# Attention heads scheduled by half after each value chunk, two start-up tables loaded from another queue, one row turn a unit earlier

## The reference, cut to what matters

```python
qkv = (h @ w_qkv).reshape(b, rows, GRID_W, 3, N_HEADS, HEAD_DIM)
q = qkv[0] * (1.0 / math.sqrt(HEAD_DIM));  k = qkv[1];  v = qkv[2]
scores = einsum(q_r, k_band) + relative bias, masked to a window
p = softmax(scores);  out = einsum(p, v_band)
x = x + out @ w_o
```

## Time and profile before

| what | value |
|---|---|
| median of 3 runs | 2391.72 us |
| the profiled execution | 2390.82 us |
| its span, first to last instruction | 2389.0 us |
| PE busy | 2336.6 us (98% of the span) |
| DVE busy | 1747.0 us (73%) |
| ACT busy | 1358.9 us (57%) |
| DMA | 397.43 MB, mean 166 GB/s |
| mean granted TensorE clock | 0.996 |
| PE's share of the chain that ended last | 72% (DVE 22%, issue 3%, ACT 3%) |

### The profile page before, as it was taken

How to read it: one execution, slowest core, us unless ns; L and a number is a source line. 1 busy time by engine, 2 the same in 40 slices (tenths; PEclk the granted TensorE clock), 3 DMA queues, 4 the chain that set the end, 5 groups by cost and what they waited for, 6 DMA issues and landing times.

```text
span 2389.0 us, 45199 instructions
## 1 busy us (share of the span) xinstructions
PE 2336.6 (98%) x15648; PEld 2092.1 (88%) x15648; DVE 1747.0 (73%) x3166; ACT 1358.9 (57%) x2527; POOL 42.8 (2%) x86
## 2 busy tenths in 40 slices
PE   8999999999999999999999999999999999899998
PEld 8899999999888888899999999988888887688776
DVE  5667999899755555775999899965556577667565
ACT  5655555877555555445445677755555455665554
POOL 1000000000000000000000000000000000000000
PEclk9999999999999999999999999999999999999999
DMA  7355555444566666555555544566665653246454
GB/s 242 126 175 159 169 167 167 149 141 139 178 192 192 194 193 192 168 178 175 177 173 169 154 141 141 155 199 193 201 198 176 185 171 105 71 124 196 130 158 142
DMA packets 137336, 397.43 MB, mean 166 GB/s; under 512 B 12464, under 2 KB 13808, under 8 KB 136432
## 3 DMA queue, kind: packets, MB, share of 16 engines
q1 hardware_dynamic: 134432, 384.97, 52.3%
q0 software_dynamic: 2480, 10.57, 1.3%
q10 hardware_dynamic: 288, 0.10, 0.0%
HBM read 394.54 MB, written 1.05 MB: 166 GB/s over the span
## 4 chain that ended last, share of the span: by engine, by line
PE 72%; DVE 22%; issue 3%; ACT 3%; DMA 0%; DVEq 0%; ACTq 0%; POOLq 0%; POOL 0%; SPq 0%
PE bank L1015 28%; PE bank L999 14%; PE bank L897 12%; DVE wl L1720 8%; PE bank L903 7%; PE bank L1028 4%; DVE arena L1931 1%; DVE arena L1932 1%; DVE arena L1934 1%; PE bank L956 1%; DVE arena L1933 1%; ACT wh L1335 1%; PE bank L944 1%; DVE arena L1930 1%; DVE arena L2003 1%
## 5 line engine op out<-in xcount | busy, mean ns | idle before, releaser
L1720 DVE TENSOR_TENSOR wl<-raw,wh 128x1024 fp32r<-128x1024 f32 (+1 forms) x732 | 893.6, 1222 | 492.0 <-ACT wh L1335 477.4
L1335 ACT ACTIVATE wh<-raw 128x1024 fp32r<-128x1024 f32 (+1 forms) x732 | 771.8, 1055 | 626.5 <-PE bank L1015 337.4
L999 PE MATMUL bank<-xh,wh 128*128 128x256 f32 x2048 | 512.6, 288 | 0.0
L999 PE MATMUL bank<-xl,wh 128*128 128x256 f32 x2048 | 501.5, 283 | 0.0
L999 PEld LDWEIGHTS bank<-xh,wh 128*128 128x128 f32 x2048 | 391.8, 191 | 1.4
L999 PEld LDWEIGHTS bank<-xl,wh 128*128 128x128 f32 x2048 | 392.6, 192 | 0.0
L999 PE MATMUL bank<-xh,wl 128*128 128x256 f32 x2048 | 292.6, 285 | 13.2 <-DVE wl L1720 13.2
L999 PEld LDWEIGHTS bank<-xh,wl 128*128 128x128 f32 x2048 | 262.7, 191 | 20.2 <-DVE wl L1720 18.9
L1015 PE MATMUL bank<-wh,gl 128*128 128x512 f32 x1008 | 270.1, 390 | 1.7 <-DVE gl L2058 1.7
L1015 PE MATMUL bank<-wh,gh 128*128 128x512 f32 x1008 | 269.8, 389 | 0.5 <-ACT gh L1501 0.5
L1015 PE MATMUL bank<-wl,gh 128*128 128x512 f32 x1008 | 269.5, 389 | 0.0
(11 more groups left out here) (296 smaller groups left out, 2739.2 us busy)
## 6 DMA issues: line engine op xcount, KB each, us to landing
raw<-in_w_upT SPq DMA_DIRECT2D x256, 512.0 KB, 3.5
raw<-in_w_down SPq DMA_DIRECT2D x256, 512.0 KB, 3.5
raw<-in_l_w_in SPq DMA_DIRECT2D x84, 512.0 KB, 3.6
raw<-in_peer_w_query SPq DMA_DIRECT2D x32, 512.0 KB, 4.2
raw<-in_l_w_out SPq DMA_DIRECT2D x28, 512.0 KB, 3.8
raw<-in_attn_w_qkv SPq DMA_DIRECT2D x24, 512.0 KB, 4.3
raw<-in_conv_w_in SPq DMA_DIRECT2D x24, 512.0 KB, 3.8
arena<-in_na_bias POOLq DMA_DIRECT2D x4, 1024.0 KB, 5.6
```

The costliest lines, as they stand in the source:

```text
L999: last = pe.matmul(banks[b][:, 0:SEQ], lhsT=w[part][:, k, :], rhs=x_in[xp][:, k, :], start=(k == 0 and part == 0 and xp == 0), stop=(k == ...
L1335: act.activation(wh[:, n % SPLIT, 0:kts * cols], raw[:, n % RAW, 0:kts * cols], ACT.Copy)\
L1720: tt(wl[:, n % SPLIT, 0:kts * cols], raw[:, n % RAW, 0:kts * cols], wh[:, n % SPLIT, 0:kts * cols].bitcast(F32), ALU.subtract).then_inc(lo ...
```

## The change

**Order of chunks.** `QKV_CHUNKS` becomes q0, k0, v0, q1, k1, v1. Chunks 2 and 5 are now the value chunks (copied by ACT), 0, 1, 3, 4 are q and k (copied by DVE).

**Steps of heads.** Heads 0 to 7 have one S per unit in units 9 to 16, T two units later, O one unit after that (12 to 19). Heads 8 to 15 have two S per unit in units 21 to 24, T one unit later (22 to 25), and O in units 24 (four heads), 25 and 26. The turns for `wo` stand at 17, 20, 25 and 27.

**Buffers.** The turned weights go to 6 buffers in `aux`, and the sums to `small`.

**The two start-up tables** are issued by POOL ahead of everything else that POOL does, and share one semaphore. PE's first transpose and DVE's first operation wait for both.

**The convolution's row turn** stands after unit 2 (`ROWS_EARLY`), and DVE's copy with it.

```diff
@@ -63,11 +63,11 @@
 SPLITS = ("attn", "peer0", "rescaled0", "conv", "peer1", "rescaled1", "mem", "even", "odd")
 SCALES = ("mem",)
 ROW_SCALES = ("attn", "peer0", "conv", "peer1", "mem", "between", "even", "odd", "final")
-WO_TURN, OUT_TURN, EVEN_TURN, ROWS_AFTER, ROWS_EARLY, ROWS_CONV = 30, 1, 2, 7, 2, 3
+WO_TURN, OUT_TURN, EVEN_TURN, ROWS_AFTER, ROWS_EARLY = 30, 1, 2, 7, 2
 
 
 ARENA = 32768
-L_QT, L_KT, L_V, L_BIAS, L_O, L_OT, L_PT = 0, 2048, 4096, 6144, 14336, 16384, 20480
+L_QT, L_KT, L_V, L_BIAS, L_O, L_OT = 0, 2048, 4096, 6144, 14336, 16384
 P_LOW = 16384
 P_QT, P_SC, P_KEYS, P_TOP = P_LOW, P_LOW + 4096, P_LOW + 8192, P_LOW + 10240
 C_C, C_U, C_Y, C_YT = 2048, 4096, 8192, 10240
@@ -221,13 +221,13 @@
 ODD_YT = (8, 0, 1, 2, 3, 4, 5, 6, 7)
 ODD_LATE = {2: (7, 8)}
 CONV_CHUNKS = (2, 4, 0, 3, 5, 1)
-QKV_CHUNKS = (0, 2, 1, 3, 4, 5)
+QKV_CHUNKS = (0, 2, 4, 1, 3, 5)
 WO_ORDER = ((0, 0), (1, 0), (0, 1), (1, 1), (0, 2), (0, 3), (1, 2), (1, 3))
 QKV_UNITS = 24
-NA_S = tuple(9 + a // 2 * 2 for a in range(NA_HEADS))
-NA_T = tuple(NA_S[a] + 1 + a % 2 for a in range(NA_HEADS))
-NA_O = tuple(20 + a // 2 if a < 8 else (24, 25, 26)[max(0, a // 2 - 5)] for a in range(NA_HEADS))
-NA_JOINED = (22, 24, 26, 27)
+NA_S = tuple(9 + a if a < 8 else 21 + (a - 8) // 2 for a in range(NA_HEADS))
+NA_T = tuple(NA_S[a] + (2 if a < 8 else 1) for a in range(NA_HEADS))
+NA_O = tuple(NA_T[a] + 1 if a < 8 else max(NA_T[a] + 1, 24) for a in range(NA_HEADS))
+NA_JOINED = (17, 20, 25, 27)
 NA = [(kind, a) for n in range(QKV_UNITS + 8) for kind, at in (("S", NA_S), ("T", NA_T), ("O", NA_O))
       for a in range(NA_HEADS) if at[a] == n]
 
@@ -482,7 +482,7 @@
 
         const_loaded = sem("const_loaded")
         N_CONST = 12
-        ident_loaded, gains_loaded = sem("identity_loaded"), sem("gains_loaded")
+        norm_loaded = sem("identity_and_gains_loaded")
         x_loaded = [sem(f"x{t}_loaded") for t in range(TT)]
         half_done = sem("down_first_half_done")
         landed = [sem(f"raw{s}_landed") for s in range(RAW)]
@@ -538,8 +538,7 @@
         XG = split_groups()
         s_buf = aux_view(0, 3, TT, SEQ)
         pT_buf = aux_view(1536, 2, 2 * TT, P)
-        na_s, na_pT = aux_view(0, 6, TT, SEQ), view(L_PT, NA_HEADS, 2 * TT, P)
-        na_sums = aux_view(3072, NA_HEADS, TT)
+        na_s, na_pT = aux_view(0, 6, TT, SEQ), aux_view(3072, 6, 2 * TT, P)
         ev_s, ev_pT = aux_view(0, 4, TT, SEQ), aux_view(5408, 4, 2 * TT, P)
 
         def scores_of(name, n):
@@ -548,12 +547,12 @@
 
         def turned_of(name, n):
 
-            return {"na": na_pT[:, n % NA_HEADS], "ev": ev_pT[:, n % 4], "om": pT_buf[:, n % 2]}[name]
+            return {"na": na_pT[:, n % 6], "ev": ev_pT[:, n % 4], "om": pT_buf[:, n % 2]}[name]
 
         def sums_of(name, n):
 
             at = 16 + n % 4 * 2 if name == "om" else 38 + n % 8 * 2
-            return na_sums[:, n] if name == "na" else small[:, at:at + 2]
+            return small[:, at:at + 2]
 
         gain_bc = aux_view(2560, D)
         causal = aux_view(3584, TT, SEQ)
@@ -706,6 +705,9 @@
             def const(dst, src):
                 pool.dma_start(dst, src).then_inc(const_loaded, 16)
 
+            pool.dma_start(ident[:], d["c_ident"]).then_inc(norm_loaded, 16)
+            pool.dma_start(gains[:], d["gains"]).then_inc(norm_loaded, 16)
+
             def summed_up(ins):
                 ins.then_inc(summed, 1)
                 pool.wait_ge(summed, count("summed"))
@@ -834,7 +836,7 @@
                     if after:
                         pe.wait_ge(residual_ready, 4 * (RES[after] - 1) + g + 1)
                     elif g == 0:
-                        pe.wait_ge(ident_loaded, 16)
+                        pe.wait_ge(norm_loaded, 16 * 2)
                     if not after:
                         pe.wait_ge(x_loaded[t], 16)
                     for k in range(4):
@@ -1240,11 +1242,11 @@
                     kind, a = NA[k]
                     if (kind, a) == ("S", 0):
                         pe.wait_ge(const_loaded, 16 * N_CONST)
-                        pe.wait_ge(gains_loaded, 16)
+                        pe.wait_ge(norm_loaded, 16 * 2)
                     if a % 8 == 0 and kind in "SO":
-                        for c in (2 * (a // 8), 2 * (a // 8) + 1) if kind == "S" else (4 + a // 8,):
+                        for c in (0, 1) if kind == "S" else (2,):
                             for i in range(2):
-                                wait_read(pe, J.of("qkv", 2 * c + i))
+                                wait_read(pe, J.of("qkv", 2 * (3 * (a // 8) + c) + i))
                     attention("na", NA, na_heads, head_base["na"], [k])
                 for g in range(4):
                     if NA_JOINED[g] == n:
@@ -1256,7 +1258,7 @@
                         done(last, j)
 
             for c in range(6):
-                project("qkv", "TTTTNN"[c], x_in, k=2 * c, ready=norm_parts("attn"), after=lambda u: na_unit(4 * c + u))
+                project("qkv", "TTNTTN"[c], x_in, k=2 * c, ready=norm_parts("attn"), after=lambda u: na_unit(4 * c + u))
             def wo_unit(i):
                 na_unit(QKV_UNITS + i)
                 if QKV_UNITS + i == WO_TURN:
@@ -1270,7 +1272,7 @@
                 def conv_unit(u):
                     if 4 * c + u == 0:
                         turn("conv", "peer0", (2, 3))
-                    elif 4 * c + u == ROWS_CONV:
+                    elif 4 * c + u == ROWS_EARLY:
                         turn_rows("rows_conv", "conv")
 
                 project("conv_in", "T", x_in, k=2 * c, ready=norm_parts("conv"), after=conv_unit)
@@ -1590,8 +1592,6 @@
 
                 return lambda p: act.wait_ge(residual_ready, 4 * (RES[name] - 1) + p)
 
-            act.dma_start(ident[:], d["c_ident"]).then_inc(ident_loaded, 16)
-            act.dma_start(gains[:], d["gains"]).then_inc(gains_loaded, 16)
             norm_split("attn", some=(0, 1))
             highs(first_unit["qkv"])
             norm_split("attn", some=(2, 3))
@@ -1603,10 +1603,10 @@
             for n in range(QKV_UNITS + 8):
                 highs(first_unit["qkv"] + n + 1)
                 c = n // 4
-                if n % 4 == 3 and c in (4, 5):
+                if n % 4 == 3 and c in (2, 5):
                     act.wait_ge(row_scale, ROW_SCALES.index("attn") + 1)
                     for t in range(TT):
-                        evac(na_v[:, t, (c - 4) * CHUNK:(c - 3) * CHUNK], J.of("qkv", 2 * c + t), scale=token[:, t:t + 1])
+                        evac(na_v[:, t, c // 3 * CHUNK:(c // 3 + 1) * CHUNK], J.of("qkv", 2 * c + t), scale=token[:, t:t + 1])
                 attention("na", NA, na_heads, head_base["na"], na_steps(n))
                 split_x("na_oT", na_out, some=[g for g in range(4) if NA_JOINED[g] == n])
                 if n == WO_TURN - 1:
@@ -2146,7 +2146,7 @@
                 step(dve.tensor_copy(rows, bank(j)[:, 0:SEQ]))
                 read_out(dve.nop(), j)
 
-            dve.wait_ge(gains_loaded, 16)
+            dve.wait_ge(norm_loaded, 16 * 2)
             for g in range(2):
                 whole("attn", g)
             for g in range(2):
@@ -2177,13 +2177,13 @@
                 c = n // 4
                 if n == ROWS_EARLY:
                     row_copies("rows_attn")
-                if n % 4 == 3 and c < 4:
+                if n % 4 == 3 and c in (0, 1, 3, 4):
                     by_token = rows.unsqueeze(1).to_broadcast([P, 2, SEQ])
                     for k in range(2):
-                        j, i = J.of("qkv", 2 * c + k), 4 * (c // 2) + 2 * k
+                        j, i = J.of("qkv", 2 * c + k), 4 * (c // 3) + 2 * k
                         wait_filled(dve, j)
                         pair = bank(j)[:, :].rearrange("p (a b) -> p a b", a=2)
-                        if c % 2 == 0:
+                        if c in (0, 3):
                             read_out(stt(na_q[:, i:i + 2, :], pair, HEAD ** -0.5, by_token, ALU.mult, ALU.mult), j)
                         else:
                             read_out(tt(na_k[:, i:i + 2, :], pair, by_token, ALU.mult), j)
@@ -2197,7 +2197,7 @@
             step(dve.memset(u[:, :, SEQ + 1:SEQ + 2], 0.0))
             cT, y = view(C_C, KT, SEQ), view(C_Y, KT, SEQ)
             conv = first_unit["conv_in"]
-            lows(conv + ROWS_CONV)
+            lows(conv + ROWS_EARLY)
             row_copies("rows_conv")
             step(tt(rows_squared, rows, rows, ALU.mult))
             for h in range(2):
```

## The result

The changed kernel is slower: 2410.80 us (median of 4 runs, 2410.59 to 2411.49) against 2391.31 beside it, a ratio of 1.008 [1.0063, 1.0096]. The forecast was 2398.6 in a range up to 2401.3: the sign was right, the size 12 us short. Timed again later, it took 2409.43 against 2391.93, 1.0071 [1.0057, 1.0085].

The account below looks back on a forecast made before the run. PE was taken to bound the attention layer (busy 122.05 of 123 us), transfers the start. Terms 5.2 (waits) + 0.5 (step changes) + 1.2 (start) + 0 (row turn) = 6.9 us, giving a median of 2398.6 us, range 2394.0 to 2401.3.

Parts of the forecast that it names:

- waits, heads 8 to 15: Attention units 21 to 24: PE waits for ACT's copies and the pairs' softmax, costing 5.2 us, the largest term.
- more changes of step: Attention on PE: singles in place of pairs add four more groups of S and O, 0.5 us, at most 0.9.
- start: Kernel start: PE's first transposes wait for both tables from POOL, making the chain 1.2 us late to the end.
- row turn: Convolution: POOL ends its row scale 0.27 us before PE ends unit 2, so no wait, 0 us; up to 0.5 if late.
- The walk: Attention units 21 to 24: PE, DVE and ACT stepped through; stage 24.05 us against 18.7 without waits.
- a unit in 12 to 19 carries one S ... 0.54: Attention, heads 0 to 7: weight unit with one S, T and O takes 2.86 + 0.54 + 0.42 + 0.88 = 4.7 us of PE.
- The sign that the prediction set for itself: Attention: the prediction is wrong if single S, T and O make a unit longer than 4.9 us.
- The start: T: Kernel start: time when both tables have landed and PE's g0 may begin; 5.2, 6.6 or 8.0 possible, 6.5 us taken.
- the prediction's own formula: Kernel start: g0 takes 0.8 us, so the chain to the first weight unit is late by T + 0.8 - 6.12.
- the late rival: Kernel start: POOL's queue serves the tables behind the crowd, T = 8.0, 1.5 us more, 2400.1; chance 0.08.
- PE's slow first matmuls go: First weight unit: rows of 1.05 us drop to 0.64, up to 1.6 us back, 2391.4; the faster rival, chance 0.05.
- The offset stays after `wo`.: After `wo` to the end: both traces run in parallel, 6 to 7 us apart, through the convolution's row turn.

Follow-up runs that it names:

- the order alone: Kernel before with only the new order of chunks and heads; start-up tables stay on ACT, row turn after unit 3: 2406.82 us, ratio 1.0064; again 2406.22, 1.0063.

## Why the prediction was wrong

The sum was 6.9 us; 19.5 were measured. Two steps carry most of the difference: one head's S was priced at half of a pair's (0.54 for 1.06 us), and PE was taken to go on at full pace behind each wait.

| step | predicted | shown |
|---|---|---|
| waits, heads 8 to 15 | 5.2 | 2.04 + 0.17 + 1.57 = 3.8, and 1.0 in gaps |
| more changes of step | 0.5 | 4.7 (singles in the old order; 4.5 in the new one) |
| PE slow behind the waits | none | 1.4 + 1.7 + 1.3 = 4.4 |
| start | 1.2 | 2.8 on the median, 2.2 to 2.3 like with like |
| row turn | 0 | some 0.8, with the new order only |

- **The walk held.** The value copy as the gate of the first `wo` unit (2.0 predicted, 2.04), the third O as the second (1.8 more than O 1 and 2 alone would let it: 1.57), no PE wait behind units 9 to 20, all with the releasers that were named. The gaps are an S and T at 105.44 to 108.00 that take 2.56 where 1.94 is enough (0.6), and the first two O (0.4).
- **The step that failed first: "a unit in 12 to 19 carries one S ... 0.54".** I halved a pair. No row of before had a single S, and I gave this term no bound of its own: it lay between 0.54 and 1.07, and eight times the difference is 4.2 us. The upper end was the truth. The sign that the prediction set for itself, a unit with single S, T and O longer than 4.9, came: 5.41, of which S is 1.06 for 0.54, T 0.49 for 0.42, O 0.81 for 0.88 and the weight unit 3.05 for 2.86. That last difference costs nothing: units 12 to 19 are of the form with 256 columns, which takes 3.05 ahead of an S in the kernel before too, and the 2.86 was read from the other form.
- **The step that was missing: what PE does after a wait.** I added up waits and resumed at full pace. The three long pieces behind the two waits cost more than the waits, 4.4 against 3.8: the unit 4.35 for 2.94, the O 3.44 for 1.76, the next unit 4.19 for 2.86. With fillers in both waits the stretch became 4.8 shorter, against 4.7 of slow rows in the profile of the order alone: all of it came back.
- **The start: T was too small.** I took 6.5; the gains landed at 7.3, 5.3 us after an issue that began at 2.02 and not at 1.52. By the prediction's own formula that makes the chain 2.0 late, and the first unit was 2.2 late. The Trainium skill (DMA: Bandwidth & Descriptors, Anatomy of one DMA — SWDGE (gpsimd) path) has 2.0 us plus bytes over 436e3, by which I estimate some 2.1 for this table; the trace disagrees, with 5.3 in the crowd of x and the weights. 7.3 lies about midway between the 6.5 I took and the 8.0 of the late rival.
- **"PE's slow first matmuls go"** looked right in the two profiles, and was not a gain of the change: they come and go with the code unchanged.
- **"The offset stays after `wo`."** In the profiles it grew from 15.0 to 18.0. The row turn is one part, 0.8. The rest lies within what the same code varies by: from POOL's scale behind the attention to that of the convolution it takes 836.8 to 838.0 us (the changed kernel's profile 837.88, before's 836.87), and from there to the end, in profiles of the old order, 1405.9 to 1409.9.

Of the 14.4 of the stretch in the two profiles, 4.7 + 3.8 + 1.0 + 4.4 = 13.9 are named.

## What to carry to other kernels

A step cut in two is not two halves: before pricing one, ask whether its matmuls ran beside one another, and where no row shows the half, carry the whole as a bound. On a PE that never waits, a new wait costs more than its length, here about twice as much where the rows behind it ran slow; look at the granted clock and at the first rows behind it, and compare a schedule with a few waits to one with none, not to the sum of the waits. A difference of 1 or 2 us between two single profiles must be checked against a third of the same code; a stretch that repeats to some hundredths, as from the first S to the row scale in the old order, is the better ruler.
